# Moving output projections into attention tails, gates beside queries, and table loads ahead in a two-block transformer kernel

## The reference

```python
# first block, layer i: attention, projection, gated FFN, per-layer embedding
h = h + mix @ w_o                       # layer 0: differential, layer 1: latent (MLA), 16 heads of 128
h = h + (silu(g) * a) @ w_out           # a, g from a width-3 convolution of rms_norm(h) @ w_in
h = h + (p_i @ w_proj) * sigmoid(rms_norm(h) @ w_gate)

# second block, layer 0 ("a"): grouped queries with rotary positions; x and context both go on
yx = (softmax(q k_all) v_all * silu(z)) @ w_out;  yc = the same for the context
x, ctx = x + g_x * yx, ctx + g_c * yc
# second block, layer 1 ("b"): each row of 64 tokens attends all rows, within a window of
# 16 columns and with a bias, and the context
px = hx @ w_in;  q, k, v, z = split(px);  kc, vc = context's
o = softmax([q k_window + bias, q kc]) [v; vc]
x = x + g_x * ((o * silu(z)) @ w_out)
return x * rsqrt(mean(x * x) + eps) * final_norm_g
```

## Time and profile before

| | |
|---|---|
| median of 3 runs | 1422.12 us (1417.61 to 1423.18) |
| profiled execution, its own time | 1420.74 us |
| its span | 1418.9 us |
| mean granted clock of PE | 0.981 |
| busy share PE / DVE / ACT / POOL | 93 / 64 / 48 / 26 % |
| weight splits, high (ACT) and low (DVE) | 295 each, mean 1057 and 1322 ns |

### The profile page before, as it was taken

One profiled execution on the slowest core, in us unless ns is written; L12 is line 12 of the kernel. 1 busy time (PEld: TensorE's weight loads), 2 busy tenths in 40 slices (PEclk: granted clock), 3 DMA queues, 4 the chain that ended last, 5 costly groups with the idle time before them and its releaser, 6 DMA issues.

```text
span 1418.9 us, 24879 instructions
## 1 busy us (share of the span) xinstructions
PE 1317.7 (93%) x9164; PEld 1150.6 (81%) x9164; DVE 910.9 (64%) x1398; ACT 683.4 (48%) x1191; POOL 369.1 (26%) x388
## 2 busy tenths in 40 slices
PE   6989999999998999898999999999989898999777
PEld 4867799999988886798999999788745578889446
DVE  6858667777766887557777778354277437533864
ACT  5554445555544776435555545234376324124651
POOL 5921134333332050232433342111011210000011
PEclk9999999999999999999999999999999998999999
DMA  8565546655643542264656664132200353334100
GB/s 291 177 223 173 181 134 210 183 185 178 182 128 104 164 138 86 102 213 135 218 179 180 186 192 169 60 104 90 89 16 1 83 154 91 103 104 134 30 1 30
DMA packets 52367, 191.58 MB, mean 135 GB/s; under 512 B 6016, under 2 KB 6272, under 8 KB 51904
## 3 DMA queue, kind: packets, MB, share of 16 engines
q1 hardware_dynamic: 43344, 158.85, 36.0%
q0 software_dynamic: 8368, 31.33, 7.1%
q10 hardware_dynamic: 576, 0.31, 0.1%
HBM read 189.41 MB, written 1.05 MB: 134 GB/s over the span
## 4 chain that ended last, share of the span: by engine, by line
PE 76%; DVE 10%; issue 7%; ACT 5%; POOL 1%; DMA 1%; SPq 0%; ACTq 0%; DVEq 0%; POOLq 0%
PE G L394 14%; PE G L396 13%; PE G L395 13%; PE A L394 5%; PE A L396 5%; PE A L395 5%; PE R L514 4%; PE R L559 3%; DVE WL L951 2%; ACT WH L1529 2%; DVE SM L1017 1%; PE A L859 1%; PE R L394 1%; PE G L923 1%; PE R L396 1%
## 5 line engine op out<-in xcount | busy, mean ns | idle before, releaser
L951 DVE TENSOR_TENSOR WL<-RAW,WH 128x1024 fp32r<-128x1024 f32 x295 | 388.2, 1322 | 339.5 <-ACT WH L1529 339.2
L1529 ACT ACTIVATE WH<-RAW 128x1024 fp32r<-128x1024 f32 x295 | 310.4, 1057 | 474.0 <-PE G L396 351.2
L394 PE MATMUL G<-XH,WH 128*128 128x256 f32 (+1 forms) x1408 | 423.7, 301 | 22.6 <-DVE XL L1310 7.5
L395 PE MATMUL G<-XL,WH 128*128 128x256 f32 (+1 forms) x1408 | 420.3, 298 | 0.0
L396 PE MATMUL G<-XH,WL 128*128 128x256 f32 (+1 forms) x1408 | 420.3, 298 | 0.0
L394 PEld LDWEIGHTS G<-XH,WH 128*128 128x128 f32 x1408 | 271.0, 192 | 34.7 <-issue 14.6
L395 PEld LDWEIGHTS G<-XL,WH 128*128 128x128 f32 x1408 | 270.9, 192 | 7.6
L396 PEld LDWEIGHTS G<-XH,WL 128*128 128x128 f32 x1408 | 270.9, 192 | 7.6
L394 PE MATMUL A<-HH,WH 128*128 128x256 f32 x352 | 99.8, 283 | 0.0
L395 PE MATMUL A<-HL,WH 128*128 128x256 f32 x352 | 99.6, 283 | 0.0
L396 PE MATMUL A<-HH,WL 128*128 128x256 f32 x352 | 99.6, 283 | 0.0
(11 more groups left out here) (321 smaller groups left out, 2266.6 us busy)
## 6 DMA issues: line engine op xcount, KB each, us to landing
RAW<-in_wst SPq DMA_DIRECT2D x295, 512.0 KB, 3.7
M<-in_wmod POOLq DMA_DIRECT2D x48, 512.0 KB, 4.6
B<-in_rpb POOLq DMA_DIRECT2D x4, 1024.0 KB, 10.8
H<-in_x_t SPq DMA_DIRECT2D x2, 512.0 KB, 9.2
M<-in_x_tok SPq DMA_DIRECT2D x1, 1024.0 KB, 12.8
M<-in_ctx_t POOLq DMA_DIRECT2D x1, 1024.0 KB, 5.2
out_y<-M SPq DMA_DIRECT2D x1, 1024.0 KB, 3.9
C<-in_cst SPq DMA_DIRECT2D x1, 737.0 KB, 14.7
```

Of the source, the lines that this page charges most:

```text
L394: mm(out, lh, rh, start=start, stop=False, skip_group_check=True)
L395: mm(out, lh, rl, start=False, stop=False, skip_group_check=True)
L951: v.tensor_tensor(WL[:, slot, :], RAW[:, raw, :], WH[:, slot, :].bitcast(F32), ALU.subtract).then_inc(w_lo, 1)
L1529: act(WH[:, slot, :], RAW[:, raw, :], ACT.Copy).then_inc(w_hi, 1)
```

## The change

1. `head_unit` is new on PE: the first unit of an output projection is issued in pieces (one k tile, one output tile, three matmuls), each once its head's output is ready, into the score banks `A`, which the attention no longer needs. Some pieces stand in the attention's tail, the rest behind it: for layer 1 4 and 3 of 32, for a 2 and 2 of 8 (of 512 columns), for b 6 and 3 of 16. DVE reads `A` instead of `G` for that unit.
2. The gates `b_z` move from behind the values to behind the queries, in the stream of panels and on all engines. ACT waits for the low half of the context's input ahead of them, since gates and that buffer share memory.
3. The scores of the last attention's first two units, with their maximum, exponential and scaling, stand within the second value unit. The last copies of values come in another order.
4. The last unit of `b_o` is two halves in two banks. Each unit's squares are summed on PE as soon as they are there; the last ones are made by ACT, half by half. The final gain is multiplied by ACT, the factor by DVE (five tiles) and POOL (three), and the output leaves in three DMAs.
5. Activation tables are loaded earlier, by a dummy activation on one column (`load_table`): the root's at the very start (where a copy stood), in the last steps of each attention and behind the last sigmoid of each embedding stage; the exponential's before the second attention. Silu stands ahead of the exponential at the start.

```diff
-          ("b_q", 8), ("b_k", 8), ("b_v", 8), ("b_z", 8), ("b_o", 8)]
+          ("b_q", 8), ("b_z", 8), ("b_k", 8), ("b_v", 8), ("b_o", 8)]
...
+            def head_unit(tag, order, width, ready):
+
+                kt = max(k for _, k in order) + 1
+                done = 0
+                for n, (c, k) in enumerate(order):
+                    i = c * kt + k
+                    pe.wait_ge(w_hi, START[tag] + i // PT + 1)
+                    pe.wait_ge(w_lo, START[tag] + i // PT + 1)
+                    ready(k)
+                    wh, wl = wtile((START[tag] + i // PT) % SPL, i % PT)
+                    dst = A[c][:, 0:width]
+                    if width == 2 * T:
+                        dst = dst.rearrange("p (a t) -> p a t", a=2)
+                        xk, xr = X2H[:, k, :, :], X2L[:, k, :, :]
+                    else:
+                        xk, xr = XH[:, k, :], XL[:, k, :]
+                    m = mm3(dst, wh, wl, xk, xr, k == 0, k == kt - 1)
+                    left = [c2 * kt + k2 for c2, k2 in order[n + 1:]] + [len(order)]
+                    now = min(left) // PT
+                    if now > done:
+                        m.then_inc(w_used, now - done)
+                        done = now
+                    yield
+
+            def advance(unit, n):
+
+                for _ in range(n):
+                    next(unit, None)
+
+            def attention(s, scores, value, filler=0, behind=None, meanwhile=(0, 0), first=0, last=None, ready=()):
                 units = attn_units(s)
                 width = 1 if s == "l0" else 2
-                for n in range(len(units) + 3):
+                for n in range(first, len(units) + 3 if last is None else last):
+                    if behind is not None and n > len(units):
+                        advance(behind, meanwhile[n - len(units) - 1])
...
                     if 2 <= n <= len(units) + 1:
                         nk = units[n - 2][2]
                         a = AU0[s] + n - 2
+                        for u, copied in ready:
+                            if n - 2 == u:
+                                pe.wait_ge(tm_v, copied)
                         pe.wait_ge(at_p, a + 1)
...
-            attention("l1", scores_l1, value_l1)
+            first_o = head_unit("l1_o", [(0, k) for k in range(14)] + [(1, k) for k in range(8)] + [(0, 14), (0, 15)]
+                                + [(1, k) for k in range(8, 16)], T, lambda k: pe.wait_ge(at_g, AJ0["l1"] + k // 2 + 1))
+            attention("l1", scores_l1, value_l1, 0, first_o, (4, 3))
+            advance(first_o, 32)
             pe.wait_ge(at_g, AJ0["a"])
-            for u in range(4):
+            for u in range(1, 4):
                 gemm_unit(U0["l1_o"] + u, START["l1_o"] + 4 * u, 0, 16, 0, 2)
                 if u == 2:
...
-            for u in gemm_wide("a_o", 8):
+            first_o = head_unit("a_o", [(0, k) for k in range(KD)], 2 * T, lambda k: pe.wait_ge(at_o, 2 * k + 2))
+            attention("a", scores_a, value_a, 0, first_o, (2, 2))
+            advance(first_o, KD)
+            for u in gemm_wide("a_o", 8, None, 1):
                 pass
...
+            for u in range(4):
+                gemm_unit(U0["b_z"] + u, START["b_z"] + 2 * u, 0, KD, 0, 2)
             for u in gemm_wide("b_k", 8, XS["bc"]):
...
+                    if k == 1 and midway is not None:
+                        midway()
...
-            evacuated(pe, U0["b_z"] + 2)
-            evacuated(pe, U0["b_z"] + 3)
-            pe.wait_ge(tm_v, TVALS + 12)
-            attention("b", scores_b, value_b)
-            pe.wait_ge(at_o, AT_JOBS["a"] + AT_JOBS["b"])
-            for u in range(4):
+            def first_scores():
+
+                pe.wait_ge(tm_v, TVALS + 8)
+                attention("b", scores_b, value_b, last=2)
+
+            value_unit(0)
+            evacuated(pe, U0["b_k"] + 6)
+            evacuated(pe, U0["b_k"] + 7)
+            value_unit(1, first_scores)
+            first_o = head_unit("b_o", [(c, k) for c in range(2) for k in range(7)] + [(0, 7), (1, 7)], T, lambda k: pe.wait_ge(at_o, AT_JOBS["a"] + k + 1))
+            attention("b", scores_b, value_b, 0, first_o, (6, 3), first=2, ready=((0, TVALS + 10), (1, TVALS + 12)))
+            advance(first_o, 2 * KD)
+            for u in range(1, 3):
                 gemm_unit(U0["b_o"] + u, START["b_o"] + 2 * u, 0, KD, 0, 2)
-            row_stats("fin")
+                row_stats("fin", R, range(u - 1, u))
+            for c in range(2):
+                p = START["b_o"] + 6 + c
+                take(p)
+                for j in range(KD):
+                    wh, wl = wtile(p % SPL, j)
+                    m = mm3(A[2 + c][:, 0:T], wh, wl, XH[:, j, :], XL[:, j, :], j == 0, j == KD - 1)
+                m.then_inc(w_used, 1)
+                if c == 0:
+                    row_stats("fin", R, range(2, 3))
+            row_stats("fin", R, range(3, 4), True)
...
-                    v.tensor_tensor(H[:, 2 * u:2 * u + 2, :], H[:, 2 * u:2 * u + 2, :], two(U0[tag] + u),
+                    v.tensor_tensor(H[:, 2 * u:2 * u + 2, :], H[:, 2 * u:2 * u + 2, :],
+                                    AA[:, 0:1024].rearrange("p (a t) -> p a t", a=2)[:, :, 0:T] if tag == "l1_o" and u == 0 else two(U0[tag] + u),
...
-                g = G[(U0["a_o"] + u) % 2]
+                g = G[(U0["a_o"] + u) % 2] if u else A[0]
...
-            attention("b", bias_b, out_b)
+            attention("b", bias_b, None, 0, 2)
+            scaled("b", 2)
+            ahead(START["b_v"] + 7)
+            attention("b", bias_b, out_b, 2, None, 2)
             for u in range(4):
                 e = START["b_o"] + 2 * u + 2
                 ahead(e)
-                used(e)
+                if u < 3:
+                    used(e)
                 g = G[(U0["b_o"] + u) % 2]
                 for c in range(2):
                     t = 2 * u + c
-                    v.scalar_tensor_tensor(H[:, t, :], g[:, c * T:(c + 1) * T], MD[:, 1, 0, 16 + t:17 + t], H[:, t, :],
+                    if u == 3:
+                        used(e - 1 + c)
+                    out = A[c][:, 0:T] if u == 0 else A[2 + c][:, 0:T] if u == 3 else g[:, c * T:(c + 1) * T]
+                    v.scalar_tensor_tensor(H[:, t, :], out, MD[:, 1, 0, 16 + t:17 + t], H[:, t, :],
                                            ALU.mult, ALU.add).then_inc(h_upd if c == 0 else bank_free[(U0["b_o"] + u) % 2], 1)
             row_factor("fin", 0)
-            for k in range(KD):
-                v.scalar_tensor_tensor(XT_OUT[:, k, :], H[:, k, :], col("fin", k), RST[:, 0, :], ALU.mult,
-                                       ALU.mult).then_inc(out_t, 1)
+            for k in range(5):
+                dv.wait_ge(out_g, k + 1)
+                v.tensor_tensor(XT_OUT[:, k, :], XT_OUT[:, k, :], RST[:, 0, :], ALU.mult).then_inc(out_t, 1)
 
...
+                act(SM[:, warmed[0]:warmed[0] + 1], EPSC, function)
+                warmed[0] += 1
...
+                    if n == len(units):
+                        load_table(ACT.Sqrt)
...
-            act(SM[:, 34:35], EPSC, ACT.Copy)
+            load_table(ACT.Sqrt)
...
+                    if u == 3:
+                        load_table(ACT.Sqrt)
...
+                if u == len(TOKEN) - 1:
+                    load_table(ACT.Exp)
...
+            ac.wait_ge(x_lo, XS["bc"])
+            for u in range(4):
+                e = START["b_z"] + 2 * u + 2
+                ahead(e)
+                ac.wait_ge(w_used, e)
+                act(flat2(ZB, u), G[(U0["b_z"] + u) % 2][:, :], ACT.Silu).then_inc(bank_free[(U0["b_z"] + u) % 2], 1)
...
                 e = START["b_v"] + 4 * g + 4
+                if g:
+                    attention("b", None, 0, 2)
                 ahead(e - 1)
-                for tt in range(4):
+                for tt in (2, 3, 0, 1) if g else range(4):
                     if tt < 3:
                         ac.wait_ge(tm_mm, len(FIRST) + len(TOKEN) + 9 + 3 * g + tt + 1)
                     else:
...
-            attention("b")
+                if g == 0:
+                    ahead(e)
+            attention("b", None, 2)
             for u in range(4):
                 ahead(START["b_o"] + 2 * u + 2)
...
+                if u:
+                    evacuated(ac, U0["b_o"] + u - 1)
+                    for t in range(2 * u - 2, 2 * u):
+                        act(XT_OUT[:, t, :], H[:, t, :], ACT.Copy, scale=col("fin", t)).then_inc(out_g, 1)
+            for c in range(2):
+                if c == 0:
+                    ac.wait_ge(h_upd, 28)
+                else:
+                    evacuated(ac, U0["b_o"] + 3)
+                act(ATP[:, 1, c * T:(c + 1) * T], H[:, 6 + c, :], ACT.Square).then_inc(fin_sq, 1)
+            for t in range(6, 8):
+                act(XT_OUT[:, t, :], H[:, t, :], ACT.Copy, scale=col("fin", t)).then_inc(out_g, 1)
             root("fin", 0, D)
+            ac.wait_ge(out_t, 5)
```

(12 more changed lines are left out.)

100 lines of the change are left out of this document (47 added, 53 removed).

## The result

The changed kernel took 1405.64 us (median of 4 runs, 1403.59 to 1406.51), against 1420.43 for the kernel before beside it; ratio 0.9892, 95% interval 0.9875 to 0.991, which is 13 to 18 us. The forecast was 1406. The profiled execution has a span of 1404.7, 14.2 less.

The account below looks back on a forecast made before the run. TensorE, busy 1317.7 of 1418.9 us, bounds the kernel, so only its idle stretches and the output's end can give time. Terms sum to 14.5 us off 1420.74: 1406 us, range 1401 to 1414.

Parts of the forecast that it names:

- The tails: Ends of the second, third and last attention: projection pieces fill PE's idle time, gaining 2.8, 3.2 and 2.8 us.
- no idle time of over 0.5 us: Sign expected on PE in the last steps of three attentions and before their first projections.
- The last attention's start: Two units of scores within the second value unit shorten the 13.5 us start by 5.0, bounds 2.7 to 6.1.
- The output: After the last projection matmul: 10.4 us to the end, 1.0 gained in all, bounds -2.3 to +3.5.
- POOL's three scalings: Final scalings on POOL beside five on DVE: 2.7 us taken, between 1.6 and 4.4.
- The three inline sums: Sums of the first three pairs on PE between the last projection's units: 3 x 0.94 = 2.8 us.
- +0.5 and +1.0: Gains from early table loads: the root's at the start (+0.5), the one moved into the first attention's tail (+1.0).
- under 0.3: Sign expected: under 0.3 us of PE wait at 168.57's place, behind the first attention, where 0.98 stood.
- -0.3: Behind the first gate stage: table load before ten casts, mostly hidden in idle ACT, costs 0.3 us, bounds -1.5 to 0.
- -1.5: Second attention's start: table load and dummy ahead of a weight split delay the first softmax by 1.5 us.
- rival (b): Table loads drain ACT's pipeline for another 1.28 us each, so two exposed loads cost 2.6 more: 1409 us; chance 8%.
- the dip: Granted clock 0.66 at 1371 to 1376, last attention's tail; costs some 1.6 us, assumed to stay.

Follow-up runs that it names:

- e5_one_dma: The changed kernel with one output DMA of 1 MB behind all eight scalings in place of three; 11.68 us end against 10.63, median 1411.62 us, ratio 0.9926.

## Why the prediction was right

**The tails.** Forecast 2.8, 3.2 and 2.8; the runs with empty tails gave 3.3, 3.2 (2.7 in the second profile) and 2.7. The first was too low because a bracket counts from the end of a row, and without a wait the next row begins before that end: the row at 588.92 is 0.60 long, and the piece behind it begins 0.36 after its start. That is 0.24 at this place, and the tail has three waits. One sign of the prediction failed, "no idle time of over 0.5 us" in the last steps: ahead of each tail's first piece PE still waits 1.2, 1.3 and 2.0, as before; no term had counted these.

**The last attention's start.** Forecast 5.0 with 1.1 us left idle; measured 4.4 on average and 5.2 between the first two profiles, 0.25 + 0.46 left idle. Gates alone gained nothing, as forecast.

**The output.** The end, 10.4 forecast, took 10.6. POOL's three scalings took 2.63 (forecast 2.7, bounds 1.6 to 4.4), DVE's five 3.35 and not 2.4: the first and the last took 0.41 to 0.42, the three beside POOL's 0.94 to 0.95. So dividing this work gained nothing: all eight on DVE had taken 3.3. (The prediction's 8 x 0.476 = 3.8 adds up lengths that overlap.) The last DMA took 3.2 and not 2.7. The three inline sums cost 0.87 each (the next projection matmul starts 0.68 later, and the one behind it another 0.19), and the first 0.75 more for the slow square: 3.4 against 2.8.
The Trainium skill's estimate ("DMA: Bandwidth & Descriptors", section "Anatomy of one DMA — SWDGE (gpsimd) path") was 2.6 for 256 KB and 4.4 for 1 MB. From issue to landing the traces have 2.8 for the last 256 KB, with two other pieces under way, and 3.9 for 1 MB in `e5_one_dma` (3.2 and 4.25 to the end of the span), so less hangs on the bytes than by that page; its figures are for DMAs issued by GpSimd, and these were issued by SP and ACT.

**What the sum missed.** The last projection came out 1.5 longer and not equal: the sums cost 3.4 and not 2.8, and against the kernel before the tail gave 1.9 and not 2.8. The missing term in the tail is 1.0 us that the change made itself: one weight split of DVE, formerly made ahead of the last attention (at 1316.3), now falls beside POOL's last rounding (0.40 became 1.32) and moved the wait before the projection from 1.79 to 2.80, of which the pieces cover 2.0.
The Trainium skill ("Trainium Architecture — The Big Picture", section "What this means for kernel authors") says that of the engines' SBUF ports only the pair of DVE and GpSimd contends, as an exclusive lock. The rows agree with it within 0.15 us: the POOL operation at 1370.27 grew by 0.92 beside a split of 1370.12 to 1371.34, the one at 1377.61 by 1.04 beside one of 1377.56 to 1378.79, and the scalings above took turns, one every 0.87 us on either engine.

**The tables.** +0.5 and +1.0 forecast, 0.9 to 1.0 measured together: the 0.53 of the earlier trace rows is gone, and the 0.98 of the earlier trace rows became 0.61, where the prediction wanted under 0.3. -0.3 came out as -0.2, within the scatter of that stage, and -1.5 as -0.9 to -1.4. No load had a drain behind it: where it had nothing else to wait for, the next activation began 0.01 us after the load's 1.28 (543.91 to 545.21; at two loads 0.17), so rival (b) fell. The load at the end, which I put at 0, gave 1.3; it is part of the 3.4 of the end.

**The clock.** I left the dip of the earlier trace rows in the forecast, "since what went ahead of the dip is not changed". That step failed: with all three places filled no profile has a lowered stretch there, at the third attention's end or at the last one's start. But the dip was no fixed part of the kernel before either: one of its three profiles has it there, the others have theirs at the third attention's end. Over all executions the span times the mean granted clock is 1390.3 before (25 executions) and 1378.4 after (5): 11.9 less. The spans themselves differ by 15.2 (1419.7 and 1404.5). The 3 us between are less time at the lowered clock. How much of them the change gives is less certain than the stages: the loss was 29.4 on average before, 26.1 after and 25.9 over the 29 executions with all three places filled, but the kernels among these lie between 23.1 and 29.9.

So the mechanism was right in most terms, and that the median lay within 0.4 us of the forecast was luck: the terms were put too high by 2.5 to 3 us (14.5 against 12), and the clock, which the sum left out, gave 3 back.

**Open.** Why an unfilled tail is followed by a lowered stretch at the third attention in three profiles and at the last in the others isn't settled, nor why none follows at the second attention, whose longest wait was 1.48; five profiles show that, not the rule behind it.

## What to carry to other kernels

Work that an in-order engine does anyway, cut into pieces and put where it waits, gains the waits at nearly their full length, and here no profile with the waits at the last two attentions filled had a lowered clock there. Before a table load or a split is moved "out of the way", look at what stands behind it on its own engine and on the engine that it feeds: both of mine had the first softmax step there, and moving it on only passed the wait to the next step. Where the clock scatters executions by more than an edit is worth, compare stages between the same instructions, with the loss to the clock taken off, not medians.

## What the runs showed of the hardware

- Over 25 executions of before the span scattered by 2.3 us (standard deviation), span times mean granted clock by 1.4: much of the scatter between executions is the clock's.
- A 128x512 fp32 product on POOL took 1.04 us alone and 2.08 when a DVE weight split of 1.23 began 0.05 us before it.
- Fp32 products of two 128x256 tiles on DVE took 0.41 to 0.42 us alone and 0.94 to 0.95 beside POOL's of the same size, which took 0.90.
- An output DMA took 2.8 us from issue to landing for 256 KB and 3.9 for 1 MB.
